# Reading back packed token rows: another queue, other places, earlier positions, and one room filled in halves

## The reference

```python
def hier_moe(h, wg, bg, we, be, w1, w3, w2):
    ...
    grp = jnp.argmax(coarse, axis=-1)
    ...
    top_v, top_i = lax.top_k(fine_g, TOPK_FINE)      # two experts of 8 in the token's group
    weight = p_grp * jax.nn.softmax(top_v, axis=-1)
    ...
    def expert_block(args):
        xi, e = args
        hid = jax.nn.silu(xi @ w1[e]) * (xi @ w3[e])
        return hid @ w2[e]
```

## Time and profile before

| what | value |
|---|---|
| median of 3 runs | 1329.2 us (1328.51 to 1332.69) |
| the profiled execution: its own time, its span | 1330.42 us, 1328.6 us |
| busy share PE, DVE, ACT, POOL | 93%, 28%, 17%, 9% |
| moved by DMA | 502.13 MB, mean 378 GB/s |
| chain that ended last | PE 61%, DMA 29%, DVE 6% |
| first expert stage (first to last `gate_up`) | 237 to 686 us |
| second expert stage | 869 to 1310 us |

### The profile page before, as it was taken

How to read it: one execution, slowest core, us unless ns; L and a number is a source line. 1 busy time by engine, 2 the same in 40 slices (tenths; PEclk the granted TensorE clock), 3 DMA queues, 4 the chain that set the end, 5 groups by cost and what they waited for, 6 DMA issues and landing times.

```text
span 1328.6 us, 18945 instructions
## 1 busy us (share of the span) xinstructions
PE 1237.5 (93%) x8035; PEld 708.6 (53%) x8035; DVE 374.9 (28%) x924; ACT 221.7 (17%) x499; POOL 116.9 (9%) x147
## 2 busy tenths in 40 slices
PE   6999999999999999988988999999999999989898
PEld 3444467655555455544545456765555555545454
DVE  3574864301021010111014884330101101111012
ACT  2223432401111110101110024230101010010001
POOL 2002000320030130030000010010000000000000
PEclk9999999999999999999998999999999999999999
DMA  9994876899999999999999873779999999999995
GB/s 367 407 347 127 319 321 247 343 427 428 427 426 429 427 427 428 427 427 429 427 424 408 310 267 139 297 314 427 427 427 427 428 427 427 427 427 428 428 426 225
DMA packets 54137, 502.13 MB, mean 378 GB/s; under 512 B 4944, under 2 KB 6232, under 8 KB 23200
## 3 DMA queue, kind: packets, MB, share of 16 engines
q1 hardware_dynamic: 50160, 493.05, 89.1%
q0 software_dynamic: 2304, 5.11, 1.3%
q10 hardware_dynamic: 1584, 2.69, 0.5%
HBM read 493.47 MB, written 7.36 MB: 377 GB/s over the span
## 4 chain that ended last, share of the span: by engine, by line
PE 61%; DMA 29%; DVE 6%; ACT 1%; issue 1%; SPq 0%; DVEq 0%; ACTq 0%; PEldq 0%
DMA ring<-in_moe_w 22%; PE B L891 22%; PE B L909 11%; PE A L919 5%; DMA both<-in_moe_w 5%; PE A L806 4%; PE B L710 4%; PE B L723 2%; PE B L653 2%; DMA ring<-in_ada_w 2%; PE B L617 2%; PE B L606 1%; DVE work L1545 1%; PE B L1159 1%; DVE work L1231 1%
## 5 line engine op out<-in xcount | busy, mean ns | idle before, releaser
L891 PE MATMUL B<-ring,work 128*64 128x256 f32 x2592 | 306.7, 390 | 13.3 <-DMA ring<-in_moe_w 13.2
L891 PEld LDWEIGHTS B<-ring,work 128*64 128x64 f32 x2592 | 182.0, 134 | 127.8 <-issue 15.7
L909 PE MATMUL B<-ring,work 128*64 128x512 f32 x880 | 199.2, 595 | 10.7 <-DMA ring<-in_moe_w 9.9
L1539 DVE TENSOR_TENSOR work<-work,B 128x256 f32<-128x256 f32 x64 | 39.5, 617 | 581.0 <-PE B L891 581.0
L919 PE MATMUL A<-work 128*128 128x256 f32 x512 | 118.2, 384 | 16.0 <-DVE work L1545 16.0
L909 PEld LDWEIGHTS B<-ring,work 128*64 128x64 f32 x880 | 61.3, 136 | 117.0 <-issue 95.2
L919 PEld LDWEIGHTS A<-work 128*128 128x128 f32 x512 | 94.9, 190 | 35.3 <-issue 23.9
L1961 ACT COPY work<-B 64x512 f32<-64x512 f32 x64 | 37.2, 581 | 458.0 <-PE B L909 458.0
L1545 DVE COPY work<-B 64x512 f32<-64x512 f32 x64 | 43.7, 683 | 199.3 <-PE B L909 199.3
L2233 POOL COPY work<-work 128x512 f32 x60 | 36.9, 615 | 697.7 <-PE B L891 655.3
L1953 ACT ACTIVATE work<-B 128x256 f32<-128x256 f32 x64 | 24.5, 383 | 324.8 <-PE B L891 324.8
(11 more groups left out here) (304 smaller groups left out, 1070.8 us busy)
## 6 DMA issues: line engine op xcount, KB each, us to landing
ring<-in_moe_w SPq DMA_DIRECT2D x136, 2048.0 KB, 32.2
work<-in_moe_w SPq DMA_DIRECT2D x25, 2048.0 KB, 32.9
ring<-in_ada_w SPq DMA_DIRECT2D x24, 2048.0 KB, 19.8
both<-in_moe_w SPq DMA_DIRECT2D x21, 2048.0 KB, 33.3
early<-in_moe_w SPq DMA_DIRECT2D x10, 2048.0 KB, 31.7
ring<-in_ev_w_in SPq DMA_DIRECT2D x6, 2048.0 KB, 18.8
ring<-in_od_w_in SPq DMA_DIRECT2D x4, 2048.0 KB, 15.8
ring<-in_ev_w_out SPq DMA_DIRECT2D x2, 2048.0 KB, 16.7
```

The source lines that it names most:

```text
L891: ins = pe.matmul((B5, B6)[m][64 * h:64 * h + 64, FH * m:FH * m + FH], xs[:, k, :], w[:, k, :].rearrange("p (q h j) -> p h q j", h=2, j=2) ...
L909: ins = pe.matmul(B7[64 * m:64 * m + 64, :], hidTb[:, k % 2, k // 2, :], w[:, k, 512 * m:512 * m + 512], start=(k == 0), stop=(k == KF - 1))
L1539: dve.tensor_tensor(hid[:, :].rearrange("p (j q) -> p q j", j=2), silu_a[:, 0:FH].rearrange("p (q j) -> p q j", j=2), B6[:, FH:FF].rearran ...
```

## The change

Four things are changed, in both layers.

1. **The queue and the places of the read-back.** It leaves SP's queue. ACT waits for `rows_out` right behind `copy_head` and issues five DMAs (`ROW_PARTS`): blocks 0 and 1 of the rows to the two blocks of `htok`, block 2 to `y2`, and the two halves of block 3 to the second half of `ph` and to `work[4096:4608]`, which is the last part of `xgp`. These places are free at that time. `copy_second` and the first `silu` now stand behind this wait and these five issues.
2. **The room in two parts.** The first half of `both` (`hT`) is free once the output projection is done (`wout_done`). Ahead of `FIRST_LOADS` SP now loads the first 1 MB of the matrix that goes to `both`, and the second 1 MB where the whole load stood, behind the same wait for the transposes.
3. **Positions.** DVE makes the integers of `first` and of `second` as soon as each is known, ahead of `Sh`; POOL waits for each pair by itself. PE's `pack_head` waits for the third signal, which is still the one behind `Sh`.
4. **The memset.** DVE's clearing of the last columns of `xgp` moves behind the transposes and its own copies (block 3 lies there until then), and POOL's `expert_rows` waits for it.

```diff
+ROW_READS = 5
...
-            count[s] += 1
+            count[s] += 1 + ROW_READS
...
+        ROW_PARTS = [(htok[:, 0, :], 0, D), (htok[:, 1, :], 0, D), (y2, 0, D),
+                     (ph[:, 1].rearrange("p a b -> p (a b)"), 0, D // 2), (work[:, SLOT:SLOT + D // 2], D // 2, D)]
...
-                if n in ROWS_THEN:
-                    sp.wait_ge(packed, 10 * (ROWS_THEN.index(n) + 1))
...
                     if at == FIRST_LOADS[l]:
-                        sp.wait_ge(packed, 10 * l + 2)
-                        sp.wait_ge(rows_out, 64 * (l + 1))
-                        sp.dma_start(rows[:, :, :], rows_d.rearrange("(b p) d -> p b d", p=P)).then_inc(slot_full[BOTH_ROOM], 16)
-                    load(n, rooms[slot(n)], src)
+                        e0, m0 = MOE_ORDER[ROWS_THEN[l] - N_MOE[l]]
+                        sp.wait_ge(wout_done, 4 * (l + 1))
+                        sp.dma_start(both[:, 0:SLOT // 2], (w1, w3, w2)[m0][NE * l + e0][:, 0:SLOT // 2]).then_inc(slot_full[BOTH_ROOM], 16)
+                    if n == ROWS_THEN[l]:
+                        sp.wait_ge(packed, 10 * (l + 1))
+                        sp.dma_start(both[:, SLOT // 2:], src[:, SLOT // 2:]).then_inc(slot_full[BOTH_ROOM], 16)
+                    else:
+                        load(n, rooms[slot(n)], src)
...
-                        ins = pe.transpose(A4[:, (f + 2) % 4, P * b:P * b + P], rows[:, b, P * f:P * f + P], ident)
+                        part, lo, _ = ROW_PARTS[b + (b == 3 and f >= 4)]
+                        ins = pe.transpose(A4[:, (f + 2) % 4, P * b:P * b + P], part[:, P * f - lo:P * f - lo + P], ident)
...
-                pe.wait_ge(packed_map, 2 * l + 1)
+                pe.wait_ge(packed_map, 3 * l + 3)
...
+                dve.tensor_scalar(placei[:, 0:TT], first[:, :, 0], -1.0, None, ALU.add).then_inc(packed_map, 1)
                 stt(second, both, -1.0, first, ALU.add, ALU.subtract)
+                dve.tensor_copy(placei[:, TT:2 * TT], second[:, :, 0]).then_inc(packed_map, 1)
...
-                tell(packed_map)
-                ts(first, first, -1.0, None, ALU.add)
-                dve.tensor_copy(placei[:, 0:TT], first[:, :, 0])
-                link(dve.tensor_copy(placei[:, TT:2 * TT], second[:, :, 0]))
...
-                            dve.memset(xgp[:, :, 2 * TOK:], 0.0)
...
+                            dve.wait_ge(packed, 10 * (l + 1))
+                            dve.memset(xgp[:, :, 2 * TOK:], 0.0).then_inc(packed_dve, 1)
...
+                act.wait_ge(rows_out, 64 * (l + 1))
+                for b, (part, lo, hi) in zip((0, 1, 2, 3, 3), ROW_PARTS):
+                    act.dma_start(part, rows_d[P * b:P * b + P, lo:hi]).then_inc(slot_full[BOTH_ROOM], 16)
                 copy_second()
...
-                    pool.wait_ge(packed_dve, 4 * l + 4)
+                    pool.wait_ge(packed_dve, 5 * l + 5)
...
-                pool.wait_ge(packed_map, 2 * l + 2)
                 for a_ in range(2):
+                    pool.wait_ge(packed_map, 3 * l + a_ + 1)
```

More of the change, by code:

```diff
@@ L160, in build @@
         htok = both[:, KD * TOK:].rearrange("p (t d) -> p t d", t=TT)
-        rows = both[:, :].rearrange("p (b d) -> p b d", b=2 * TT)
         brow = sb("brow", [48 * LAYERS, P])
@@ L865, in rows_transposed @@
                     if f >= 4:
-                        pe.wait_ge(packed_act if f % 2 else packed_dve, (7 * l + 3 if f % 2 else 4 * l) + f // 2 - 1)
+                        pe.wait_ge(packed_act if f % 2 else packed_dve, (7 * l + 3 if f % 2 else 5 * l) + f // 2 - 1)
                     for b in range(2 * TT):
-                        ins = pe.transpose(A4[:, (f + 2) % 4, P * b:P * b + P], rows[:, b, P * f:P * f + P], ident)
+                        part, lo, _ = ROW_PARTS[b + (b == 3 and f >= 4)]
+                        ins = pe.transpose(A4[:, (f + 2) % 4, P * b:P * b + P], part[:, P * f - lo:P * f - lo + P], ident)
                     ins.then_inc(packed, 1)
```

## The result

The changed kernel is slower, by less than one per cent, where 6.8 us less were forecast.

What follows compares the result with a forecast made beforehand. Transfers were taken to bound both expert stages' ends. Half room plus earlier restart less holes gave 4.0 us in the first layer and 2.8 in the second, together 6.8, forecasting 1322.4 us, range 1319.0 to 1327.0.

Steps and rivals of the forecast that it cites:

- PE's delays: Start of both expert stages: PE about 1.1 and 4.3 us late, costing only where this makes holes in the stream.
- the holes: Weight stream early in each expert stage: gaps from late-freed rooms, taken as 0.4 us and 2.6 us.
- the half room: Both layers: 1 MB of weights moved into the idle stretch before the scatter, gaining 2.5 us a layer, 4.9 us in all.
- the earlier restart of the stream: After the scatter: transfers resume at 241.2 instead of 243.1 us and about 873.5 instead of 876.4, gaining 1.9 and 2.9 us.
- the hold: ACT's wait and five issues delay the first silu; PE stands 1.3 us in the first layer, 3.4 in the second.
- (d): Slower rival: PE does not catch up within a stage and sets the end; 5.4 us more, 1334.6 us, chance 0.04.
- my signs of being wrong: ACT's issues near 1 us, dips longer than 3 us, or the second stage's chain staying with PE to the end.
- What bounds the kernel: Both expert stages: the end is the stream's start, plus its bytes at 426 GB/s, plus holes; PE catches up.
- Positions: Both layers: integers made earlier let POOL's scatter start and end 1.9 us earlier.
- The clock: Second layer, after PE's 3.4 us idle: a stretch at 1.2 GHz costing 1.0 us; none in the first layer.
- The rule that I held not to apply: Row reads on ACT: by the rule only 0.38 us of issue time is saved, and the 1.9 and 2.9 us are missing.
- rival (b): Read-back on ACT: the queue gains nothing, data start no earlier, only the half room counts; 1324.3 us, chance 0.06.

Runs made afterwards that it cites:

- e1: The changed kernel with SP's further weight loads held until all five row reads have landed: 1330.26 us, ratio to the kernel before 0.9996.
- e3: The changed kernel with the three weight loads after the row reads in each layer cut into 4 KB pieces: 1328.8 us, ratio to before 0.9976.
- e8: The changed kernel with ACT's copy_second and first silu put ahead of its wait and row reads: 1346.85 us, ratio to before 1.0112.
- e10: The kernel of e8 with the three following weight loads of each layer cut into 4 KB pieces: 1333.64 us, ratio to before 1.0023.
- e2: The changed kernel with the scatter wait and five row reads back on SP's queue, ahead of the next weight load: 1323.4 us, ratio to before 0.9942.
- e9: The kernel of e2 measured again in more rounds: 1324.8 us, ratio to before 0.9953.
- e4: The kernel before with the early positions alone, read-back on SP's queue, whole room: 1328.05 us, ratio to before 0.9977.
- e6: The kernel of e2 without the half room, both filled whole behind the transposes: 1328.42 us, ratio to before 0.9979.
- e5: The kernel of e2 with ACT held by the scatter wait and eight extra copies before copy_second: 1327.11 us, ratio to before 0.9972.

## Why the prediction was wrong

**The step that failed** is the sentence "The rows share the engines with one weight load; together they need 9.8 us and end by 252 and 884 us, ahead of PE's transposes". They ended at 262 and 898.5 us. In the first layer PE stood 7.16 us for them; in the second PE was later still. Two things were wrong in it. I added bytes, as if the later of two transfers only had to wait for the sum; but the engines deal in packets, and the rows' were four to eight times smaller. And I counted one weight load, where SP issued three before the rows were down (in the first layer (3,0), (3,1), (2,2), at 242.1, 245.7 and 252.0 us), so that the competition went on for as long as the rows did. Before the change all of this stood in one queue, rows first. That order was worth more than the wait in it, and I had treated leaving it as a pure gain. e1 (no load beside) and e3 (equal packets) take away 10 and 11 us by this cause, and e8 against e10 shows it a second time, 13 us.

**What followed from it** had the mechanism that the prediction gave for PE's delays, at another size: rooms come free late, and the stream, which I had seen to be short of margin, runs dry. The terms of the sum for the holes were 0.4 and 2.6 us; the missing transfer measured 10.0 and 5.0 us. With them the sum comes out near what was measured: 2.5 us for the half room, 2.3 and 2.1 us for the earlier restart of the stream (3.3 us behind the start of the stage instead of 5.6, and 5.6 instead of 7.7; the forecast had 1.9 and 2.9), less the holes, is -5.2 and -0.4 us, against -5.4 and -1.5. The second layer's hole has another source than the first's: the hold, and a stretch of half clock that cost 6.36 - 3.85 = 2.5 us where I took 1.0. The rival that I named for a slower kernel, (d), was another mechanism, and it did not occur: in the changed kernel the chain still turns to transfers, at 464 and 1203 us, before both stages end (the time of 3 and 7 experts later than before, where I said 4 to 6). Of my signs of being wrong it was the dips longer than 3 us that came. No rival had the rows themselves come late.

**What bounds the kernel** was read rightly. e2 and e9 gain 7.0 and 6.8 us, where 8 to 9 us were expected of e2; that the sum for the change was 6.8 too is chance.

**Positions** were forecast at 3.8 us and gave 2.4 to 3.1 (e4). **The half room** was forecast at 4.9 and gave 3.6 (e6 to e9). The terms are right in kind and look a fifth to over a third too large, which is within the scatter of these runs.

**The hold of ACT** was forecast as 1.3 and 3.4 us of idle PE and was 1.46 and 4.01; its price, 3.0 us in the sum, was 2.3 (e5). ACT's five issues took 2.4 us in the first layer and 3.1 in the second, where I took 2.0.

**The clock.** I expected one stretch of 3.4 us at 0.50 and none in the first layer. The changed kernel has 6.8 us in each (from 259.7 and 887.7 us); the one in the first layer begins while PE stands the 7.16 us for the rows, which I had not foreseen.

**The rule that I held not to apply**, that a second issuing engine saves only the time of the issue (the Trainium skill, DMA: Bandwidth & Descriptors, "Issuing engines are not separate DMA queues"), would have been the better guide, though the 4.9 us that I priced it at, as rival (b), were wrong as well. The early start did come, 1.6 us for the reads in the first layer, but e2 has nearly all of it on SP's queue too. What ACT's queue added was only that the weights no longer had to stay behind the rows.

**Still open** is the spread of the changed kernel's runs, 1327.4 to 1346.3 us, against 1328.5 to 1332.7 before. e8, where the weights are there from the start of the reads, has 1344.0 to 1347.3 in four runs. It would fit that the start that the rows have over the weights (4.3 us in the profiled execution's first layer, none in e8) differs from run to run, but only one execution of each is profiled, so this is argued and not shown.

## What to carry to other kernels

Think twice before a transfer that someone waits for goes on a queue of its own beside bulk loads that are free to go. Count the packets on both sides, for in these runs the bytes were shared in the ratio of the packet sizes, and look for every load that can be issued before the wanted one is down, not only for the next. With one queue and the urgent transfer first, the rows were down in 8 us instead of 18 to 22; where a transfer must run beside others, cutting the others to its packet size got it down in 13 to 17 us. When a wait stands in a queue and seems to cost, ask what order it keeps before it is taken out.

## What I had not expected of the hardware

**Packets one to one.** Two queues with work were served packet for packet over stretches of 6 to 12 us (279 to 279 in e8, 185 to 185 in the changed kernel), with packets from 2 to 16 KB. A packet here is a single piece, not a whole transfer.

**A late first packet.** On idle engines the data of ACT's first read followed its issue by 1.0 us (240.46 us, then 241.5). With a weight load issued on SP's queue just before, it took 2.5 us in the second layer of the changed kernel (880.52 to 883.0, the load at 880.37), and 4.0 us in e8 (883.16 to 887.2, the load at 882.56). In e8 these are all the packets between 883.6 and 887.1 us:

```profile
DMA packets 70, 1.15 MB, mean 328 GB/s; under 512 B 0, under 2 KB 0, under 8 KB 0
```

They are all of the weights' size, none of the rows'. It goes the other way round as well: in the changed kernel's first layer the rows were issued first, and the weight load of 242.10 us brought its first packet at 245.75, 3.7 us later. What holds the first packet back was not looked into.
